# Forget attention by pairs of heads: scores on half the array's rows each, and the causal mask merged with the decay into a bias

## The reference, cut to what matters

```python
q, k = rmsnorm(q, q_gain), rmsnorm(k, k_gain)      # per head, 64 wide
cum = cumsum(log_sigmoid(x @ w_f + b_f))           # (head, token)
# for every block of 128 queries t, over keys s <= t:
logits = q @ k.T * 64 ** -0.5 + cum[t] - cum[s]
out = softmax(where(causal, logits, -inf)) @ v
```

## Time and profile before

| | us |
|---|---|
| median of 3 runs | 2099.71 (2099.28 to 2102.07) |
| the profiled execution | 2096.7 |
| its span, first to last instruction | 2095.0 |
| TensorE busy | 2017.3 (96%) |
| VectorE, ScalarE, GpSimd busy | 977.2, 451.0, 337.5 |
| mean granted clock of TensorE | 0.985 |

### The profile page before, as it was taken

How to read it: one execution, slowest core, us unless ns; L and a number is a source line. 1 busy time by engine, 2 the same in 40 slices (tenths; PEclk the granted TensorE clock), 3 DMA queues, 4 the chain that set the end, 5 groups by cost and what they waited for, 6 DMA issues and landing times. The chain is left out here.

```text
span 2095.0 us, 20480 instructions
## 1 busy us (share of the span) xinstructions
PE 2017.3 (96%) x7494; PEld 1087.0 (52%) x7494; DVE 977.2 (47%) x1817; ACT 451.0 (22%) x1094; POOL 337.5 (16%) x474
## 2 busy tenths in 40 slices
PE   8999999999999999999899999999998999999994
PEld 4444444579884444444445457554444557544442
DVE  2444535557773024333454656343344467444333
ACT  1112111023342001100241136220004446320000
POOL 1000000000102000334200013103331003203333
PEclk9999999999999999999999999999999999999997
DMA  5223365610012234599816850047995120046996
GB/s 183 90 101 130 109 249 186 215 66 2 1 50 92 79 102 160 219 405 400 301 62 216 312 192 2 14 168 304 403 391 183 63 103 2 3 161 226 372 375 243
DMA packets 123511, 363.32 MB, mean 173 GB/s; under 512 B 27596, under 2 KB 33000, under 8 KB 110864
## 3 DMA queue, kind: packets, MB, share of 16 engines
q1 hardware_dynamic: 77856, 174.13, 23.4%
q10 hardware_dynamic: 30432, 157.30, 19.2%
q0 software_dynamic: 15120, 30.53, 4.2%
HBM read 335.60 MB, written 43.52 MB: 181 GB/s over the span
## 5 line engine op out<-in xcount | busy, mean ns | idle before, releaser
L1617 PE MATMUL bank<-ring,work 128*128 128x512 f32 x768 | 342.5, 599 | 3.3 <-DVE work L1633 3.3
L1617 PEld LDWEIGHTS bank<-ring,work 128*128 128x128 f32 x768 | 144.1, 193 | 167.8 <-issue 167.8
L1916 POOL DMA_INDIRECT work<-x_rows,small x168 | 169.1, 1007 | 269.5 <-DVE work L1881 197.4
L1628 PE MATMUL bank<-ring_halves,work 128*128 128x512 f32 x384 | 172.9, 593 | 4.0 <-DVE work L1642 4.0
L432 PE MATMUL bank<-featT,ring 128*128 128x512 f32 x384 | 170.3, 597 | 2.8 <-DMA ring<-in_w_in 2.8
L2404 PE MATMUL bank<-ring,featT 128*128 128x512 f32 x384 | 168.9, 601 | 1.6 <-DVE small L2493 1.6
L1345 PE MATMUL bank<-ring,work 128*128 128x512 f32 x384 | 166.5, 593 | 3.5 <-PEq L2186 2.4
L1639 DVE TENSOR_TENSOR work<-work,bank 128x256 f32<-128x256 f32 x48 | 20.2, 420 | 282.4 <-ACT work L1636 282.4
L2404 PEld LDWEIGHTS bank<-ring,featT 128*128 128x128 f32 x384 | 73.7, 193 | 93.8 <-issue 92.0
L1628 PEld LDWEIGHTS bank<-ring_halves,work 128*128 128x128 f32 x384 | 72.8, 190 | 95.0 <-issue 95.0
L1345 PEld LDWEIGHTS bank<-ring,work 128*128 128x128 f32 x384 | 72.3, 190 | 91.6 <-issue 91.6
(11 more groups left out here) (444 smaller groups left out, 2826.7 us busy)
## 6 DMA issues: line engine op xcount, KB each, us to landing
ring<-in_w_in SPq DMA_DIRECT2D x15, 2048.0 KB, 12.5
ring<-in_moe_w_gate ACTq DMA_DIRECT2D x28, 1024.0 KB, 6.9
ring<-in_moe_w_up ACTq DMA_DIRECT2D x28, 1024.0 KB, 9.9
ring_halves<-in_moe_w_down ACTq DMA_DIRECT2D x28, 1024.0 KB, 10.2
ring_halves<-in_w_ada SPq DMA_DIRECT2D x48, 512.0 KB, 6.4
y_rows<-work ACTq DMA_DIRECT2D x48, 512.0 KB, 10.3
ring<-in_expert_w_gate ACTq DMA_DIRECT2D x14, 1024.0 KB, 7.9
ring<-in_expert_w_up ACTq DMA_DIRECT2D x14, 1024.0 KB, 10.9
```

The lines of the kernel that those rows point to most:

```text
L1617: last = nc.tensor.matmul(gu_sum[par], xgT[par][:, k, :], w_gu[par][:, k, :, :], start=(k == 0), stop=(k == KD - 1))
L1628: last = nc.tensor.matmul(bank[5 + h][:, :], hT[par][:, k, :], w_dn[par][:, k, span(h)], start=(k == 0), stop=(k == KF - 1))
L1916: nc.gpsimd.indirect_dma_start(out=xg[par][:, s * QD:(s + 1) * QD], out_offset=None, in_=x_quarters, in_offset=bass.IndirectOffsetOnAxis(a ...
```

## The change

Queries and keys are 64 wide again. The running sums are turned into rows by four transposes of TensorE at job 14 (`sums_by_row`), stored in DRAM by GpSimd, and loaded back for each head as four rows, broadcast over all 128 partitions, one for each t (`load_bias`). GpSimd writes the causal triangle into each (`select`, an affine select of 128x128). The bias so made is what VectorE's pass now adds in place of the mask. Four sets of bias tiles are used in turn. Heads 0 and 1 are loaded by GpSimd during the projections, the others by SP in the attention's own stage; from head 4 on each load waits for VectorE's last pass over the set's older head.

The forget attention gets a function of its own. Its step is one t of both heads of a pair (32 steps, indices 2j and 2j+1 for the two heads). One transpose turns a block of both heads' queries or keys (128 wide). The scores of the two heads use rows 0 to 63 and 64 to 127 of the array, and four score banks in turns of two. Shares are turned three steps behind their scores (`TURN_LAG`), each head into one bank of its own; ScalarE copies those of the first head and VectorE those of the second; the value products come five steps behind (`PV_LAG`), into one output bank. The reciprocals of both heads are one instruction, the output copy is ScalarE's. GpSimd's queue has twelve selects (heads 0 to 2) ahead of the first share, and then two selects ahead of each share in the steps named by `select_at`.

```diff
-        FW = FD + 1
-        QKV = T * NHB * FW
-        qkv_f = [work[:, i * QKV:i * QKV + T * NHB * n].rearrange("p (t h n) -> p t h n", t=T, h=NHB) for i, n in enumerate((FW, FW, FD))]
-        FOX_END = 2 * QKV + T * DM
+        qkv_f = [work[:, i * T * DM:(i + 1) * T * DM].rearrange("p (t h n) -> p t h n", t=T, h=NHB) for i in range(3)]
+        FOX_END = 3 * T * DM
...
+        f_rows = work[0:NHB, F0 + 928:F0 + 928 + S]
+        key_rows = nc.dram_tensor("key_rows", [NHB, S], F32, kind="Internal").ap()
+        rows_stored, bias_landed, first_bias_landed = sem("key_rows_stored"), [sem(f"bias_landed{i}") for i in range(4)], [sem(f"first_bias_landed{i}") for i in range(2)]
+        B0 = FOX_END + 2 * 2 * S
+        SEG = [P * (t + 1) for t in range(T)]
+        bias_at = [[work[:, B0 + o:B0 + o + n] for o, n in zip((0, 128, 384, 768), SEG)],
+                   [work[:, o:o + n] for o, n in zip((F0, B0 + 1280, F0 + 128, B0 + 1536), SEG)],
+                   [work[:, F0 + 512 + o:F0 + 512 + o + n] for o, n in zip((0, 128, 384, 768), SEG)],
+                   [a[:, o:o + n] for a, o, n in zip((state, work, state, state), (0, F0 + 1792, 128, 512), SEG)]]
+
+        def load_bias(eng, h):
+            for t in range(T):
+                eng.dma_start(bias_at[h % 4][t], key_rows[h:h + 1, 0:SEG[t]].partition_broadcast(P)).then_inc(first_bias_landed[h] if h < 2 else bias_landed[h % 4], 16)
...
-        F_AT, CUM_AT, Q_AT, K_AT = 8, 12, 9, 17
+        F_AT, CUM_AT, ROWS_AT, Q_AT, K_AT = 8, 12, 14, 9, 17
...
-        stage(pe_n, ac_n, dv_n, ["ones_q"])
+        stage(pe_n, ac_n, dv_n)
         with nc.Block() as block:
             @block.sync
             def _(sp):
-                load(sp, gains[:, 0:1], D["fox_q_norm_2"].rearrange("o p -> p o"))
-                load(sp, gains[:, 1:2], D["fox_k_norm_2"].rearrange("o p -> p o"))
+                for m in range(2):
+                    load(sp, gains[FD * m:FD * (m + 1), 0:1], D["fox_q_norm_2"].rearrange("o p -> p o"))
+                    load(sp, gains[FD * m:FD * (m + 1), 1:2], D["fox_k_norm_2"].rearrange("o p -> p o"))
...
+                def sums_by_row():
+                    AC.wait(pe, "cum")
+                    for t in range(T):
+                        last = nc.tensor.transpose(bank[0][0:NHB, t * P:(t + 1) * P], f_cum[:, t * NHB:(t + 1) * NHB], ident[:, :])
+                    PE.done(last, "cum_rows")
 
...
-                        AC.done(nc.scalar.activation(qkv_f[1][:, :, :, FD], T4(bank[0][:, NR:2 * NR], NHB), ACT.Copy, scale=-1.0), "cum")
+                        AC.done(nc.scalar.activation(f_cum, bank[0][:, NR:2 * NR], ACT.Copy, scale=-1.0), "cum")
+                    if j == ROWS_AT:
+                        PE.wait(act, "cum_rows")
+                        AC.done(nc.scalar.activation(f_rows, bank[0][0:NHB, :], ACT.Copy), "cum_rows")
...
-                PE.wait(pool, ("sum",) + jobs[7])
-                PO.done(nc.gpsimd.memset(qkv_f[0][:, :, :, FD], 1.0), "ones_q")
+                AC.wait(pool, "cum_rows")
+                pool.dma_start(key_rows[:, :], f_rows).then_inc(rows_stored, 16)
+                pool.wait_ge(rows_stored, 16)
+                for h in range(2):
+                    load_bias(pool, h)
 
...
-        oT2 = attention(FW, *qkv_f, FOX_END, FOX_END + 2 * TURNED_HEADS * S, None, k_gain)
+        def fox_attention(q, k, v, turned_at, out_at):
+
+
+            sx = [halves_of_ring[:, i * BANK:(i + 1) * BANK] for i in range(8)]
+            scr = featT[:, :, :].rearrange("p k s -> p (k s)")
+            pT = [scr[:, i * BANK:(i + 1) * BANK].rearrange("p (s n) -> p s n", s=T) for i in range(6)]
+            turned = [[work[:, turned_at + (2 * i + m) * S:turned_at + (2 * i + m + 1) * S] for m in range(2)] for i in range(2)]
+            outT = work[:, out_at:out_at + KD * S].rearrange("p (k s) -> p k s", k=KD)
+            mx, inv = small[:, 64:128], small[:, 128:192]
+            NP = NHB // 2
+            both = range(2)
+            steps = [(p, t) for p in range(NP) for t in range(T)]
+            N = len(steps)
+            TURN_LAG, PV_LAG = 3, 5
+            END = N + PV_LAG
+            q_at = {T * (p - 1): p for p in range(1, NP)}
+            k_at = {T * (p - 1) + 2: p for p in range(1, NP)}
+            out_at_step = {T * p + T - 1 + PV_LAG: p for p in range(NP)}
+            select_at = {**{T * p - 1: 2 * p + 2 for p in range(1, NP - 1)}, **{T * p: 2 * p + 3 for p in range(NP - 1)}}
+            turn_bank, out_bank, X = (bank[4], bank[5]), bank[6], bank[7]
...
+            with nc.Block() as block:
+                @block.sync
+                def _(sp):
+                    for h in range(2, NHB):
+                        if h >= 4:
+                            DV.wait(sp, ("neg", 2 * (T * ((h - 4) // 2) + T - 1) + h % 2))
+                        load_bias(sp, h)
+
+                @block.tensor
+                def _(pe):
+                    def turn_pair(b, x, p, name):
+                        for t in range(T):
+                            last = nc.tensor.transpose(b[:, t * P:(t + 1) * P], x[:, t, 2 * p:2 * p + 2, :].rearrange("p h n -> p (h n)"), ident[:, :])
+                        PE.done(last, name)
...
+                    for j in range(END):
+                        if j in q_at:
+                            if q_at[j] == 1:
+                                AC.wait(pe, ("q", 0))
+                            else:
+                                DV.wait(pe, ("k", q_at[j] - 1))
+                            turn_pair(X, q, q_at[j], ("q", q_at[j]))
+                        if j in k_at:
+                            AC.wait(pe, ("q", k_at[j]))
+                            turn_pair(X, k, k_at[j], ("k", k_at[j]))
+                        if j >= PV_LAG:
+                            i = j - PV_LAG
+                            p, t = steps[i]
+                            AC.wait(pe, ("pT", 2 * i))
+                            DV.wait(pe, ("pT", 2 * i + 1))
+                            if t == 0 and p:
+                                AC.wait(pe, ("out", p - 1))
+                            for s in range(t + 1):
+                                for m in both:
+                                    last = nc.tensor.matmul(out_bank[FD * m:FD * (m + 1), t * P:(t + 1) * P], v[:, s, 2 * p + m, :], pT[(2 * i + m) % len(pT)][:, s, :],
+                                                            start=(s == 0), stop=(s == t))
+                            PE.done(last, ("pv", i))
+                        if j < N:
+                            p, t = steps[j]
+                            if t == 0:
+                                AC.wait(pe, ("q", p))
+                                DV.wait(pe, ("k", p))
+                            if j >= 2:
+                                AC.wait(pe, ("exp", 2 * (j - 2) + 1))
+                            qT, kT = turned[p % 2]
+                            for m in both:
+                                PE.done(nc.tensor.matmul(bank[(2 * j + m) % 4][:, 0:(t + 1) * P], qT[FD * m:FD * (m + 1), t * P:(t + 1) * P], kT[FD * m:FD * (m + 1), 0:(t + 1) * P],
+                                                         start=True, stop=True), ("S", 2 * j + m))
+                        if TURN_LAG <= j < N + TURN_LAG:
+                            i = j - TURN_LAG
+                            for m in both:
+                                PO.wait(pe, ("share", 2 * i + m))
+                                if i:
+                                    (DV if m else AC).wait(pe, ("pT", 2 * (i - 1) + m))
+                                for s in range(steps[i][1] + 1):
+                                    last = nc.tensor.transpose(turn_bank[m][:, s * P:(s + 1) * P], sx[(2 * i + m) % len(sx)][:, s * P:(s + 1) * P], ident[:, :])
+                                PE.done(last, ("turn", 2 * i + m))
+
+                def keep_turned(eng, m, i):
+                    n = steps[i][1] + 1
+                    PE.wait(eng, ("turn", 2 * i + m))
+                    if i >= len(pT) // 2:
+                        PE.wait(eng, ("pv", i - len(pT) // 2))
+                    return pT[(2 * i + m) % len(pT)][:, 0:n, :], turn_bank[m][:, 0:n * P].rearrange("p (s n) -> p s n", s=n)
+
...
+                    keep_q(0)
+                    for j in range(END):
+                        if j in out_at_step:
+                            p = out_at_step[j]
+                            PE.wait(act, ("pv", T * p + T - 1))
+                            AC.done(nc.scalar.activation(outT[:, p, :], out_bank[:, :], ACT.Copy), ("out", p))
+                        if j < N:
+                            n = (steps[j][1] + 1) * P
+                            for m in both:
+                                i = 2 * j + m
+                                DV.wait(act, ("neg", i))
+                                if i >= len(sx):
+                                    PE.wait(act, ("turn", i - len(sx)))
```

(53 more changed lines are left out.)

42 lines of the change are left out of this document (37 added, 5 removed).

## The result

The changed kernel takes 2134.2 us (median of 4 runs, 2133.3 to 2136.7); the kernel before took 2100.5 on the same chip (2099.3 to 2102.1). The ratio is 1.016, with a 95% interval of 1.014 to 1.018: slower by 34 us, outside the range of 2087 to 2106. The profiled execution took 2134.7 (span 2133.0), the one before 2096.7 (span 2095.0).

The account below looks back on a forecast made before the run. The forget attention was taken as bound by TensorE. Pairs -9.1, start +1.85, end +2.25, later heads' bias +1.0 and outside +0.5 sum to -3.5 us, so 2099.7 becomes 2096.2; range 2087 to 2106.

Parts of the forecast that it names:

- end of the stage: After the last t=3 scores: five steps of value products remain, 9.1 us in place of 6.86, a loss of 2.25.
- outside the stage: Projections: four transposes and a wait for ScalarE cost 0.5 us; loads sharing DMA with adaptation slabs, 3.5 there, cost nothing.
- Bias of the later heads: Reloads in each pair land 5.0 us behind the scores, fitting by 0.1; 1.0 us charged in all.
- the prediction's own sign of being wrong: In each pair of the attention stage, GpSimd's selects wait over 5 us.
- rival (a): Bias comes late in every pair: 1.0 us later gives 2103, 1.5 beyond the margin 2106; chance 0.16.
- TensorE's work: TensorE's own work per pair of heads in the attention: 9.06 us in place of 11.64.
- rival (b): Row halves of the two heads' scores don't overlap: 2106, or with partial overlap 2101; chance 0.08 and 0.08.
- (d): VectorE becomes the bound of the attention; with 10.5 us per pair 2099; chance 0.05.
- rival (e): Every TensorE change of tile shape costs a full tail: 0.06 more at three changes a step, 2101; chance 0.05.
- copy waits: TensorE waits twice per pair at a turn for the copy of the step before: 0.38 and 0.43 us.
- Start of the stage: TensorE stands 6 us before the first turn, then half clock for 3.2: 22.7 in place of 20.85, loss 1.85.
- rival (c): Heads 2 and 3 land early and nothing stalls at the start: 2088, or 2082 without copy waits; chance 0.18.

Follow-up runs that it names:

- own parts: Changed kernel with 1280 sums per head in DRAM, each of a head's four small loads reading its own part; 2098.0 us.
- both: One load per head, heads 2 and 3 issued by SP in the stage before, every pair's selects two steps later; 2096.5 us, ratio 0.998 to the kernel before.
- early loads: Kernel with one load per head, loads of heads 2 and 3 issued by SP in the stage before, landing behind fox_w_out; 2094.6 us.
- one load per head: Changed kernel with each head's four prefixes one behind the other in DRAM and brought by one DMA; 2095.0 us.
- filled gap: Changed kernel with 24 transposes of the identity ahead of the t=3 turn of each pair from 1 to 6; 2132.0 us.
- loads first: The kernel of both, with the loads of heads 2 and 3 really issued ahead of the second half of fox_w_out; 2090.1 us.
- scores apart: Kernel with one load per head, order changed to score and turn of the first head, then of the second; 2128.2 us.

## Why the prediction was wrong, step by step

In the profiled executions the sum should have been -3.5 and was +38.0 (2133.0 against 2095.0). The 41.5 between them are (the terms are rounded):

| step of the prediction | forecast | measured | off by |
|---|---|---|---|
| stage's start to the second pair's t=3 scores | 22.7 | 28.0 | 5.3 |
| from there to the last t=3 scores, bias included | 60.0 | 90.7 | 30.7 |
| end of the stage | 9.1 | 9.1 | 0 |
| outside the stage | 0.5 | 6.1 | 5.6 |

- **Bias of the later heads** is the step that failed. Its frame was right: release at 0.96 (0.99), two selects and a share, a margin of 0.1 behind a landing at 5.0. The landing was at 9.45, and the prediction's own sign of being wrong came: GpSimd's selects waited 7.1 to 8.5 us in each of the five pairs. I had priced "the last 262 KB and the semaphore" by bytes from the one large transfer of the earlier trace rows, and had no row of small pieces read from one place by several loads; own parts, where the first head lands 6.8 behind the scores, shows that 2.6 of the 4.45 go with that layout; the other 1.8 are simply more than I gave four small loads beside those of the next head. I took the good end of an unbounded cost and gave rival (a) 0.16 with 1.5 us as its worst; it was 4.45 late, and nothing in the earlier trace rows excluded that. A second thing was left out of its price: I charged the half clock of the earlier trace rows to the first gap and to no other, though (a) opens a gap in every pair. That is 2 of the 6 us per pair.
- **TensorE's work, 9.06 per pair.** Right in kind, a little small. The halves of the rows overlap, so rival (b) is out; so is (d), since VectorE is busy 54.9 of 87.9 us in *both*. Two heads' scores take 0.42, 0.63, 0.85 and 1.06, 2.96 in place of 2.16 + 0.56 = 2.72: 0.06 more for each group, which is rival (e)'s price at one of its three places. The copy waits were 0.44 and 0.31 (forecast 0.38 and 0.43). Without loads a pair takes 10.25 (10.0), the last 9.47 (9.0).
- **Start of the stage.** The idle time stood where it was forecast, 7.84 in place of 6, since heads 2 and 3 landed 10.4 and 14.7 behind SP's issue in place of 8.5 to 9.7 and 10.3 to 12.6. So rival (c) is out: small loads did land behind the 2 MB (in early loads 9.0 us after an issue 0.5 behind it; the median of such a load in one load per head is 4.9). The first turn came 3.6 later for it. The other 1.7 are the half clock, which lasted some 8 us behind the gap where I took 3.2 from the earlier trace rows. The Trainium skill (TensorE: Matmul & The Clock Gate, Part 4) was named ahead for a loss of 3 here; the direction is right, but its ground, that transposes don't count, isn't borne out: in filled gap 24 transposes and nothing else held the full clock.
- **End of the stage.** Right: 1357.12 to 1366.22 is 9.1.
- **Outside.** "3.5 us there, and VectorE's last slab ends 6 us before" was wrong twice. First the loads of heads 0 and 1 cost VectorE more. Its 18 slabs of one kind in the projections, first to last start, of the kernel before, the changed one, own parts and one load per head:

```profile
L286 DVE SCALAR_TENSOR_TENSOR ring_halves<-ring_halves,ismall x18: 1275/1283/1285, 1148.6 to 1226.7; 128x1024 f32<-128x1024 f32 x18
```

```profile
L286 DVE SCALAR_TENSOR_TENSOR ring_halves<-ring_halves,ismall x18: 1275/1283/1286, 1147.6 to 1233.4; 128x1024 f32<-128x1024 f32 x18
```

```profile
L286 DVE SCALAR_TENSOR_TENSOR ring_halves<-ring_halves,ismall x18: 1273/1283/1285, 1148.0 to 1232.2; 128x1024 f32<-128x1024 f32 x18
```

```profile
L286 DVE SCALAR_TENSOR_TENSOR ring_halves<-ring_halves,ismall x18: 1275/1283/1286, 1148.6 to 1230.2; 128x1024 f32<-128x1024 f32 x18
```

  That is 78.1, 85.8, 84.2 and 81.6: 7.7 more in place of 3.5. Only 1.6 of it goes when the loads read separate parts; 3.5 stays even with one load per head. Second, the slack was smaller than 6. The stage waits for the store of VectorE's last sum too (SP issues it at 1234.81, 3.1 us to landing) and begins 3.7 behind the last slab, so that of the 7.0 us in the kernel before 3.3 were free. The last slab ended at 1234.7 in place of 1228.0, 6.7 later, and so the stage began 3.4 later. The last 2.7 lie behind the stage (766.8 in place of 764.1); in the other kernels that stretch was 761.1 to 767.2, so I put them down to nothing.

What the change is worth is seen in *both*, with the bias on time: the pairs give 7.5 (60.7 in place of 68.15), the start 2.8 (18.1 in place of 20.85), and the end takes 2.25, as forecast; 8.0 in all. What turned this into a loss was delivery.

## What to carry over

When a change makes an engine wait for a transfer once in every round, work out the loop (release, landing, the waiting engine's work, the next release) and ask from which landing on it, and not the busiest engine, sets the period; if no row shows such a transfer, the far end of its price belongs in the sum's range and a later consumption costs nothing to try. Loads that may be in flight at once and begin at the same bytes in DRAM are worth a trial with bytes of their own, or as one load: here 2134.2 became 2098.0 and 2095.0. A gap on TensorE costs more than its length: price the half clock behind it each time it comes.

## What the runs showed of the hardware

- Four broadcast loads of 64 to 256 KB that begin at the same DRAM bytes: 6.1 to 7.0 us to land for 128 KB and more (medians of those into `work`), 103 GB/s for two heads. From separate parts of a longer row 3.3 to 3.7, from 128 distinct rows 2.6 to 3.9, as one load of 640 KB 4.9.
- Scores of two heads on 64 rows each take together what one takes alone (1.06 and 1.05 for 512 keys, 0.42 and 0.41 for 128).
- TensorE's granted clock fell to half (1.2 GHz) behind idle times of 2.7 to 3.3 us in each of five pairs of the changed kernel and, in loads first, behind one of 1.7 that left it at 2.4 GHz in *both*; 24 transposes of the identity in the idle time kept it at 2.4 GHz in the pair shown. In scores apart it stayed at half from 1246 to 1272 although TensorE was busy nearly all of that time.
